# First block's attentions on TensorE in pairs of units, with a third place for the turned blocks

## The reference, cut to what matters

```python
# layer 0 ("ev"): 8 heads of global attention over context + latents, and 8 heads of
# neighbourhood attention with a bias table, head size 64; latents and context as queries
p = softmax(q @ [k_ctx, k_lat].T)            # global_gqa, 512 keys; context queries: 256 keys
y = p @ [v_ctx, v_lat]
s_nb = q @ k_neighbours.T + rpb[...]         # neighbourhood_attention, latents
p = softmax([s_nb, q @ k_ctx.T]);  y = p_nb @ v_nb + p_ctx @ v_ctx
# layer 1 ("od"): 16 heads, window of 128 with a sink logit, latents only as queries
p = softmax([where(valid, q @ k_band.T, NEG), q @ k_ctx.T, sink]);  y = p[..., :-1] @ v
...
y = concat(heads) @ w_out                    # then layer norm and the convolution FFN
```

## Time and profile before

| what | value |
|---|---|
| time, median of 3 runs | 1574.95 us (1573.91 to 1576.41) |
| span of the profiled execution | 1572.0 us |
| PE busy | 98% of the span |
| DVE, ACT, POOL busy | 68%, 56%, 21% |
| share of PE in the chain that ended last | 90% |
| "ev" attention, from S3 to the first product after it | 150.53 to 223.06 us |
| "od" attention, from S3 to the first product after it | 689.63 to 738.17 us |

### The profile page before, as it was taken

One profiled execution on the slowest core, in us unless ns is written; L12 is line 12 of the kernel. 1 busy time (PEld: TensorE's weight loads), 2 busy tenths in 40 slices (PEclk: granted clock), 3 DMA queues, 4 the chain that ended last, 5 costly groups with the idle time before them and its releaser, 6 DMA issues.

```text
span 1572.0 us, 25520 instructions
## 1 busy us (share of the span) xinstructions
PE 1543.6 (98%) x9936; PEld 1319.7 (84%) x9936; DVE 1067.6 (68%) x1983; ACT 880.8 (56%) x1735; POOL 337.9 (21%) x340
## 2 busy tenths in 40 slices
PE   7999999999999999999999999999999999999998
PEld 4788778988887888887999988988888898888886
DVE  4743766666444525788787768777888668779874
ACT  2423873666652423568455555756766557567662
POOL 0201420355540000112011102242221014412210
PEclk9999999999999999999999999999999999999999
DMA  9766123345657224021545562424555534335551
GB/s 369 301 238 243 21 82 134 122 182 205 236 226 261 81 108 152 13 79 68 186 177 218 184 231 105 144 104 164 187 189 187 202 142 154 139 137 188 187 202 78
DMA packets 46951, 260.35 MB, mean 166 GB/s; under 512 B 11888, under 2 KB 13168, under 8 KB 18160
## 3 DMA queue, kind: packets, MB, share of 16 engines
q1 hardware_dynamic: 43952, 252.78, 43.7%
q0 software_dynamic: 1296, 4.72, 0.8%
q10 hardware_dynamic: 1584, 1.23, 0.2%
HBM read 257.64 MB, written 1.07 MB: 165 GB/s over the span
## 4 chain that ended last, share of the span: by engine, by line
PE 90%; DVE 4%; ACT 3%; DMA 2%; issue 1%; POOL 0%; SPq 0%; DVEq 0%; ACTq 0%
PE ps L512 22%; PE ps L513 21%; PE ps L514 21%; PE ps L764 8%; PE ps L765 5%; PE ps L667 2%; PE ps L689 2%; PE ps L676 2%; PE ps L528 2%; PE ps L1164 1%; PE ps L766 1%; DMA raw<-in_ada 1%; PE ps L575 1%; DMA raw<-in_ev_w_in 1%; PE ps L1191 1%
## 5 line engine op out<-in xcount | busy, mean ns | idle before, releaser
L1931 DVE TENSOR_TENSOR wl<-raw,wh 128x1024 fp32r<-128x1024 f32 (+2 forms) x304 | 357.5, 1217 | 249.9 <-ACT wh L1437 248.6
L1437 ACT CAST wh<-raw 128x1024 fp32r<-128x1024 f32 (+1 forms) x318 | 313.6, 1036 | 337.0 <-PE ps L514 302.3
L512 PE MATMUL ps<-xx,wh 128*128 128x256 f32 (+1 forms) x1006 | 328.1, 326 | 0.0
L514 PE MATMUL ps<-xx,wl 128*128 128x256 f32 (+1 forms) x1006 | 325.5, 324 | 0.0
L513 PE MATMUL ps<-xx,wh 128*128 128x256 f32 (+1 forms) x1006 | 325.5, 324 | 0.0
L512 PE MATMUL ps<-wh,xx 128*128 128x512 f32 (+2 forms) x780 | 285.9, 367 | 2.7 <-DVE xx L2356 1.2
L514 PE MATMUL ps<-wh,xx 128*128 128x512 f32 (+2 forms) x780 | 281.1, 360 | 0.0
L513 PE MATMUL ps<-wl,xx 128*128 128x512 f32 (+2 forms) x780 | 281.0, 360 | 0.0
L2302 DVE SCALAR_TENSOR_TENSOR arena<-ps,pv,arena 128x254 f32<-128x254 f32 (+2 forms) x352 | 192.9, 548 | 28.7 <-ACT arena L1637 19.3
L512 PEld LDWEIGHTS ps<-xx,wh 128*128 128x128 f32 x1006 | 189.9, 189 | 20.1 <-issue 4.0
L514 PEld LDWEIGHTS ps<-xx,wl 128*128 128x128 f32 x1006 | 189.9, 189 | 15.2
(11 more groups left out here) (242 smaller groups left out, 2234.9 us busy)
## 6 DMA issues: line engine op xcount, KB each, us to landing
raw<-in_ada SPq DMA_DIRECT2D x46, 1024.0 KB, 5.0
raw<-in_up SPq DMA_DIRECT2D x44, 1024.0 KB, 4.9
raw<-in_fin SPq DMA_DIRECT2D x44, 1024.0 KB, 4.8
raw<-in_down SPq DMA_DIRECT2D x22, 1024.0 KB, 4.8
raw<-in_fout SPq DMA_DIRECT2D x22, 1024.0 KB, 4.8
raw<-in_win SPq DMA_DIRECT2D x12, 1024.0 KB, 4.9
raw<-in_ev_w_in SPq DMA_DIRECT2D x9, 1024.0 KB, 7.4
raw<-in_wout SPq DMA_DIRECT2D x8, 1024.0 KB, 4.9
```

The source lines that it names most:

```text
L512: e.matmul(out, A[0], B[0], start=first, stop=False)
L514: return e.matmul(out, A[1], B[0], start=False, stop=last)
L1437: e.copy(hi_of(j)[:, a:b], raw_of(j)[:, a:b]).then_inc(*S.hi.up((j, half)))
L1931: e.tensor_tensor(lo_of(j)[:, a:b], raw_of(j)[:, a:b], hi_of(j)[:, a:b].bitcast(F), ALU.subtract).then_inc(*S.lo.up((j, half)))
```

## The change

Each of the two attentions gets a third place for turned blocks, so `turned(i)` waits for the values of unit `i-3` instead of `i-2`. On TensorE the values come one unit later than before (`i-5` instead of `i-4` in iteration `i`), and odd iterations write the blocks in another order than even ones. ACT's and DVE's `mixed_high` and `mixed_low` come one iteration later. Otherwise the queues of ACT, DVE and POOL stay as they were.

```diff
@@ class Att
+        def PT(self, i):
+            return self.PTS[i % 3]
@@ ATT: "ev", "od"
-... [AR(2048, 2, 512), AR(6656, 2, 512)]),
+... [AR(2048, 2, 512), AR(6656, 2, 512), AR(12288, 2, 512)]),
-                  [AR(13312, 2, 512), AR(0, 2, 512)]),
+                  [AR(13312, 2, 512), AR(0, 2, 512), AR(16384, 2, 512)]),
@@ tensor_program, attention1
-            for i in range(A.n + A.lag + 1):
+            for i in range(A.n + A.lag + 2):
+                if i % 2 and 0 <= i - A.lag - 2 < A.n:
+                    values(i - A.lag - 2)
+                if i % 2 and 0 <= i - A.lag < A.n:
+                    transposes(i - A.lag)
                 if i < A.n:
                     scores(i)
                     fill(i)
-                if 0 <= i - A.lag < A.n:
+                if i % 2 == 0 and 0 <= i - A.lag < A.n:
                     transposes(i - A.lag)
-                if i > A.lag:
-                    values(i - A.lag - 1)
+                if i % 2 == 0 and 0 <= i - A.lag - 2 < A.n:
+                    values(i - A.lag - 2)
@@ scalar_program, attention1
-                    if i >= 2:
-                        q.wait_ge(*S.val.at((key, i - 2)))
+                    if i >= 3:
+                        q.wait_ge(*S.val.at((key, i - 3)))
...
-                if i > A.lag + 1:
-                    mixed_high(i - A.lag - 2)
+                if i > A.lag + 2:
+                    mixed_high(i - A.lag - 3)
@@ vector_program, attention1
-                if i > A.lag + 1:
-                    mixed_low(i - A.lag - 2)
+                if i > A.lag + 2:
+                    mixed_low(i - A.lag - 3)
```

More of the change, by code:

```diff
@@ L418, in __init__ @@
         def __init__(self, key, stage, P, PT):
-            self.key, self.units, self.P, self.PT = key, units_of(stage), P, PT
+            self.key, self.units, self.P, self.PTS = key, units_of(stage), P, PT
             self.lag = len(P) - 1
             self.n = len(self.units)
+        def PT(self, i):
+            return self.PTS[i % 3]
         def slot(self, i):
@@ L471, in _build @@
     ATT = {
-        "ev": Att("ev", "ev", [P4a[:, 0, :, :], P4a[:, 1, :, :], tmp[:, :, :], AR(18432, 2, 512)], [AR(2048, 2, 512), AR(6656, 2, 512)]),
+        "ev": Att("ev", "ev", [P4a[:, 0, :, :], P4a[:, 1, :, :], tmp[:, :, :], AR(18432, 2, 512)], [AR(2048, 2, 512), AR(6656, 2, 512), AR(12288, 2, 512)]),
         "od": Att("od", "od", [AR(6656, 2, 512), AR(7680, 2, 512), AR(4608, 2, 512), AR(10240, 2, 512)],
-                  [AR(13312, 2, 512), AR(0, 2, 512)]),
+                  [AR(13312, 2, 512), AR(0, 2, 512), AR(16384, 2, 512)]),
     }
@@ L688, in values @@
                     for m in range(2):
-                        r = e.matmul(ps[b][64 * m:64 * m + 64, tk], v[m], A.PT[i % 2][:, m, 128 * j:128 * j + 128],
+                        r = e.matmul(ps[b][64 * m:64 * m + 64, tk], v[m], A.PT(i)[:, m, 128 * j:128 * j + 128],
                                      start=first, stop=last)
@@ L1489, in turned @@
                     q.wait_ge(*S.pt.at((key, i, m)))
-                    if i >= 2:
-                        q.wait_ge(*S.val.at((key, i - 2)))
-                    e.copy(A.PT[i % 2][:, m, :], ps[4 + m]).then_inc(*S.ea.up((key, "pt", i, m)))
+                    if i >= 3:
+                        q.wait_ge(*S.val.at((key, i - 3)))
+                    e.copy(A.PT(i)[:, m, :], ps[4 + m]).then_inc(*S.ea.up((key, "pt", i, m)))
             def softmax(i):
@@ L1516, in mixed_high @@
                     e.copy(xh[:, k, 0:n], ps[A.units[i]["bank"]][:, 0:n]).then_inc(*S.xh.up((key, k)))
-            for i in range(A.n + A.lag + 2):
-                if i > A.lag + 1:
-                    mixed_high(i - A.lag - 2)
+            for i in range(A.n + A.lag + 3):
+                if i > A.lag + 2:
+                    mixed_high(i - A.lag - 3)
                 if 0 <= i - A.lag < A.n:
```

## The result

The changed kernel is slower. Its median is 1584.16 us (four runs, 1581.31 to 1585.37) where the kernel before has 1575.53 (four runs); the ratio on record is 1.0047 (that of the two medians would be 1.0055), with a 95% interval of 1.0035 to 1.0059, so 5.5 to 9.3 us. The profiled executions span 1580.0 and 1572.0 us, 8.0 apart; the changed kernel's is that of its shortest run.

What follows compares the result with a forecast made beforehand. TensorE was taken to bound the kernel before, rings through ACT and DVE after. Terms of 2.7, 1.8, 0.3 and 1.4 us sum to +6.2 us, 1581.2 us in the median; range for 8 in 10: 1575.5 to 1586.

Steps and rivals of the forecast that it cites:

- What bounds: Middle of both attentions: TensorE is busy the whole time and bounds, others follow with 2 to 8% to spare.
- TensorE alone: Both attentions on TensorE: joined blocks save 3.8 us in "ev" and 2.2 in "od", 6.0 us if nobody is late.
- The ring in "ev": Middle of "ev": transposes wait for ACT's copies behind exponentials needing the pair's first scores; 58.8 us instead of 56.0, +2.7.
- The ring in "od": Middle of "od": a ring over two pairs through DVE's weights takes 13.5 us against 12.45; 32.9 against 31.1, +1.8 us.
- The ends: Start and tail of both attentions: transposes wait for copies; +0.3 us in "ev", +1.4 in "od", the least sure term.
- Sum: Whole kernel: the terms add up to +6.2 us, 1578.2 us in the profile, 1581.2 us in the median.
- The signs: Trace of "ev": transposes start 0.7 us after the copies, TensorE idling 0.1 to 1.5 us before; ACT hardly idles.
- The second: Both attentions: copies come in time and TensorE alone decides; -6.0 us, 1568 us; chance 0.10.
- The third: Both attentions: rings form only where weights or casts stand, ends free; +1 to +2.8 us, 1576 to 1577.7; chance 0.10.
- The fourth: Both attentions: DVE's and ACT's queues add up, DVE being at 95% in "od"; 1586 to 1590 us; chance 0.06.
- The fifth: TensorE's blocks: 0.15 to 0.20 us belong to a block's start, not its kind; 1583 to 1587 us; chance 0.02.
- The rule of rotating banks: Transposes share banks 4 and 5; by the skill's rule rotating PSUM banks would spare the wait, giving 1568 us.

Runs made afterwards that it cites:

- run 5: The changed kernel with ACT's copies out of banks 4 and 5 moved ahead of the odd unit's exponentials; 1582.76 us, ratio 1.0059.
- run 2: The changed kernel with an extra ACT copy of 0.52 us in even iterations 6 to 22 of "ev", directly ahead of the regular copies; 1585.89 us.
- run 3: The changed kernel with an extra ACT copy of 0.52 us in odd iterations 5 to 21 of "ev", ahead of the regular copies; 1583.0 us.
- run 4: The kernel before with an extra ACT copy of 0.52 us in even iterations 6 to 22 of "ev", ahead of the regular copies; 1574.54 us.
- run 6: The changed kernel with ACT's four halves of weights in "ev" one unit earlier, after units 14, 16, 18 and 20; 1580.41 us, ratio 1.0034.
- run 8: The changed kernel with ACT's copies first, its "ev" weights after even units and DVE's "od" low parts of weights one iteration later; 1581.39 us, ratio 1.0044.
- run 9: The changed kernel with DVE's low parts of the weights in "od" one iteration later; 1580.28 us, ratio 1.0035.
- run 12: The changed kernel with two of SyncE's four transfers of gate rows moved behind the "ev" attention; 1582.86 us, ratio 1.0048.
- run 10: The changed kernel with the edits of run 6 and run 9 together, and ACT's cast of a result behind its iteration's copies; 1578.37 us, ratio 1.0020.

## Why the prediction was right, point by point

- **What bounds.** Right. PE was busy all the time before, and what the others had to spare in sum (ACT 2 and 8%, DVE 5% in "od", but 22% in "ev") said nothing about whether they could answer within a pair.
- **TensorE alone, -6.0.** Right as a price: joined blocks stand 0.86 and 0.88 us apart where nobody waits, and pair 11 of run 5 takes 5.87 us. None of it arrived as time.
- **The ring in "ev", +2.7.** Right in mechanism (runs 2 to 4 and 6) and within 0.1 us in eight of nine pairs. The measured term is +3.8. The miss is pair 7, 0.76 us, and some 0.04 a pair in most others. The step that failed there is the link "S to maxima 1.18", which I took for the same everywhere; in pair 7 it was 1.90. Rows of before could have told: there the same instruction started 2.89 us after S7, covered by the old order.
- **The ring in "od", +1.8.** Right that it goes over two pairs and through DVE's weights (runs 8 and 9). Measured +2.24. The first round, S5 to S9, took 13.57 us and the second 13.90 instead of 13.5. The ring starts anew from every odd unit (S7 to S11 is 13.90 as well, which is why pair 9 is 6.60 and not 6.2), and from unit 7 on it has a link that the sum left out: the split of a result on DVE (L2259), which the change moves from even to odd iterations, between the maxima of o and the weights. It takes 712.04 - 711.70 = 0.34 us; in the iteration of unit 5 there is none:

```profile
705.36 0.16 DVE L2221 TENSOR_TENSOR st<-st,rows 128x2 f32<-128x2 f32 x1
705.43 1.22 DVE L1944 TENSOR_TENSOR wl<-raw,wh 128x1024 fp32r<-128x1024 f32 x1
...
711.70 0.42 DVE L2259 TENSOR_TENSOR xx<-ps,xx 128x256 fp32r<-128x256 f32 x1
712.04 1.22 DVE L1944 TENSOR_TENSOR wl<-raw,wh 128x1024 fp32r<-128x1024 f32 x1
```

Run 9 fits: its S7 to S11 takes 6.19 + 6.58 = 12.77 us, 13.90 less the 1.13 of the weights. So the ring over two pairs bounds there too, with ACT's weights and the two halves of the split still in it, and pair 9 stays at 6.58.
- **The ends, +0.3 and +1.4.** Measured 3.97 - 3.82 = +0.15 and 3.74 - 2.24 = +1.5. Within them T0 waited 1.19 us for its normalisation without moving S4, which started 4.23 us later than before, just the delay that "ev" had left. In "ev" T21 and T23 waited 0.62 and 0.28 after S23, where I had given 0.7 and 0.4, and T22 0.23.
- **Sum.** +6.2 predicted, +8.0 in the profiled execution: +1.1 from the "ev" middle, +0.4 from "od", nothing more than forecast from the ends, and 0.3 that was there ahead of the first attention. The median came 3 us over the forecast, inside the range.
- **The signs.** T started 0.7 us after the copies and waited where it was said to: 0.53 us for pair 13, 1.02 for 17 and 1.48 for 19 (0.6, 1.1 and 1.5 were given). For 15 and 21 it was 0.67 instead of 1.1, since S16 and S22 waited 0.32 first. One sign was wrong: "ACT should hardly idle there". With the same 51.6 us of work in a longer stretch ACT idled 8.3 us, in pair 19 alone 1.29, ahead of its exponentials. That follows from the prediction's own sums and doesn't touch them: the ring makes ACT wait for DVE as it makes PE wait for ACT.
- **Rivals.** The second, faster by the time that TensorE saves, needs T to run on without a wait; eight waits in "ev" exclude it. The third, rings only where weights stand and the ends free, fits "ev" in part and fails by "od" and the sum. The fourth, DVE's work adding to ACT's, was not reached in time (1586 to 1590), though the split of a result in "od" is a piece of it. The fifth is excluded by the pairs of 5.87 us.
- **The rule of rotating banks** ("Perfetto Trace Analysis", Optimizing Tensor Performance, Matmuls, in the Trainium skill) spoke against the change, and the trace agrees: all of 14 waits of T in the whole run that name the copies, 9.5 us, are for banks 4 and 5. What other banks for T would bring was not run.

What stays open: by which way small packets delay other engines (that they do rests on one profile, run 12); and how much of the runs' spread (1581.3 to 1585.4) is pair 7, which only profiled executions show. A kernel with the short rings of run 10 and without the packets at that place was not run; run 10 less the excess of its pair 7 over 6.04, 2.2 us, would still be 3.0 us behind before by this estimate.

## What to carry to other kernels

Before joining two blocks on the busiest engine, draw the ring from the first block back to itself through every in-order queue and every pair of shared banks, and add up the starts: a resource used by both blocks of a pair gives the other engines one pair's time, two units, where the order of before gave them nearly three units. With the ring longer than the pair, every microsecond in it counts in full, whatever the average load; work that must be done can stand one iteration elsewhere on the same engine for nothing (runs 3 and 9), but moving one link may put another in its place (run 5). Whatever a change moves along with the blocks belongs in the sum as well: the split of a result, one iteration later, was a link of the ring of "od". And an unexplained late start in the trace of before can be a cost that waits for its cover to go.

## What the runs showed of the hardware

- A change of the kind of matmul (64 rows, whole array, 64 columns at a time) costs TensorE 0.20 us after a block on 64 rows (1.06 against 0.86 us from start to start) and 0.15 after one of 64 columns (1.03 against 0.88); two pairs of blocks joined save 0.36 us in 6.23 (pair 11 of run 5). For the whole array no run shows the price by itself.
- Four transfers of 4 KB to memory in packets of 4 bytes (4224 packets under 512 bytes in 150:165) were followed by idle time that the profile ascribes to nobody: 1.03 and 0.66 us on PE in run 10, 0.7 us of late start on DVE and, through it, ACT and POOL in the changed kernel. With half of the packets it was gone at that place, in one profile. Two of these transfers placed beside a load of 512 KB brought its landing from 8.8 to 16.0 us, and held SyncE's queue 4.53 us.
